# Second part's first RMS norm: the factor per token moved from the inputs of the 14 products to their sums

## The chip, the cores and the metric

The kernel runs on one core of a Trainium2 chip, as one launch. The metric is the device time of that launch in microseconds (us), lower is better. All arithmetic is on 32-bit floats; a product "in three passes" splits both operands into a high part (fp32r) and a low rest and adds high·high, high·low and low·high.

## The reference, cut to what matters

256 tokens of width 1024 pass a first block (a mixer and a feed-forward layer, ended by a layer norm "ln2") and then a second block. The change concerns the hand-over:

```python
x = _layer_norm(ALPHA * h + ff, ln2_g, ln2_b)            # end of the first block
...
def rmsnorm(x, g):
    return x * lax.rsqrt(jnp.mean(x * x, axis=-1, keepdims=True) + EPS) * g
h = rmsnorm(x, g_norm1) * (1.0 + sc1) + sh1              # sc1, sh1: one value per feature
proj = h @ w_in                                          # 1024 x 1792: 14 blocks of 128 outputs
q, k, v, z = jnp.split(proj, ...)                        # 4, 1, 1 and 8 blocks
q = rmsnorm(q, g_q); k = rmsnorm(k, g_k)                 # per head; then rotation and attention
z = gelu(z)                                              # then a token-mixing layer
```

rsqrt(mean) is one factor r per token. So proj = r · (x·gain) @ w + sh1 @ w, where gain = g_norm1·(1+sc1).

## The kernel before, in words

Activations lie transposed in SBUF: features on the 128 partitions in 8 tiles, tokens along the free dimension. `xh` and `xl` are the high and low parts of a product's input, 8 tiles of 16 + 256 columns (the 16 were the meta tokens of the first block and are free in the second). All weights come as one stream of 128x1024 blocks, issued by SP through a ring of four slots: `raw` is what landed, ACT's `hi(b)` (L1082 to L1089) rounds it to `wh`, DVE's `lo(b)` (L1605 to L1610) makes `wl = raw - wh`, and PE's `block` (L750 to L762) runs 24 matmuls of 256 columns. `hi(b)` waits until block b-4 is done on PE, `lo(b)` waits for `hi(b)`, PE waits for `lo(b)`. Both are written AHEAD = 3 blocks before their use. There is no planner: each engine's order is written out by hand, and each engine works strictly in that order.

The stage in question, with n counting the 14 blocks of `w_in` (B_IN2 to B_OUT2):

- **Layer norm ln2.** Statistics per token (L1947 to L1975, L1300 to L1317), PE turns the normed rows back to feature layout in banks 4 to 7 (L738).
- **RMS norm, before.** ACT squares each tile (L1371), PE sums the squares with eight full matmuls (L804) that spread the sum over all partitions, DVE makes x·gain from PSUM (L2025), ACT takes the root (L1382), DVE the reciprocal `spread` (L2028), then for each tile DVE multiplies by it (L2038), ACT adds the shift into `xh` (L1387), DVE makes `xl` (L2033).
- **Blocks 0 and 1** run tile by tile in `first_blocks` (L507). Blocks 2 to 13 run in `block`, in PSUM banks 0 and 1 in turn.
- **Between them**, PE transposes `res` (L818) and the token-mixing weights (L810), and does parts of attention and of the token-mixing layer (L835 to L933).
- **ACT's loop** (L1459 to L1503): iteration n is `hi(n+3)`, some extras, then, once block n is done, GELU (n < 8), a copy (n = 8), or a square and a scaled copy (n > 8), all read from PSUM.
- **DVE's loop** (L2115 to L2169): iteration n is extras, `lo(n+3)`, and for n < 8 one multiply-add of `ada` over 128x1024 (L1989), which computes a later modulation vector. In iteration 3 it also copies `y_tm` (L2149) and makes a diagonal (L2152). It doesn't read the blocks' sums.

Of the kernel before, what the change touches and what calls it, by code (L numbers as in the profile page):

```python
# [5 lines left out]
F32 = mybir.dt.float32  # L6
# [6 lines left out]
P = 128  # L13
# [17 lines left out]
QT = 4  # L31
# [99 lines left out]
def two_blocks(nc: bass.Bass, A: dict, out: bass.AP):  # L131
    with ExitStack() as ctx:
# [3 lines left out]
        def sem(name):  # L136
# [146 lines left out]
        q_scale = hb[:, 16:32].rearrange("p (i t h) -> p i t h", i=QT, t=NT)  # L283
        heads2 = cst[:, C_BLK:C_BLK + P:HD]
# [21 lines left out]
            "z_act", "zv_turned", "zv_copied", "zv_ms", "zv_std", "zv_n", "mixed", "tok_pre", "tok_done", "tok_sq",  # L306
# [8 lines left out]
        NORM = {what: sem(f"r1_{what}") for what in ("sq", "var", "std", "h", "hi", "lo")}  # L315

        def norm(what, n=1):
# [4 lines left out]
                   "norm_act": (0, 0, 3, 6), "turned": (0, 8, 16, 24), "h": (0, 8, 16, 16), "hi": (0, 8, 16, 24), "lo": (0, 8, 16, 16)}  # L322
# [144 lines left out]
        def _(pe):  # L467
# [282 lines left out]
            def block(b, bank, name, value, t=0, h=xh, l=xl, first=META):  # L750
# [5 lines left out]
                for n in range(KD):  # L756
                    a, z = h[:, n, first:first + SEQ], l[:, n, first:first + SEQ]
                    w_hi, w_lo = (w[:, b % RING, n * P:(n + 1) * P] for w in (wh, wl))
                    for w, x in ((w_hi, a), (w_hi, z), (w_lo, a)):
                        mm = nc.tensor.matmul(ps[:, bank, 0:SEQ], w, x, start=(k == 0), stop=(k == 3 * KD - 1))  # L760
                        k += 1
# [45 lines left out]
            pe.wait_ge(S["mixing_landed"], 64)  # L807
            for n in range(2):
                for q in range(4):
                    mm = nc.tensor.transpose(ps[:, 2 + n, q * P:(q + 1) * P], ws[:, 4 * n + q, :], ident)  # L810
                mm.then_inc(S["ws_turned"], 1)


            def turn_y(t):

                pe.wait_ge(*ln("n2", "hi", KD))
# [145 lines left out]
            for b in range(B_IN2, B_OUT2):  # L962
                n = b - B_IN2
                c = n - 2
                if c < 0:
                    free = (None, 0)
                elif c < 2 * QT:
                    free = ("z_act", c + 1)
                elif c == 2 * QT:
                    free = ("v2_ev", 1)  # L970
                else:
                    free = ("q_ev", c - 2 * QT)
# [9 lines left out]
                if n == 5:  # L982
                    gate_row()
# [93 lines left out]
        def _(act):  # L1077
# [287 lines left out]
            token_norm("n2", F1_BANKS, eps[:, 1:2], B_IN2 - 1 + AHEAD)  # L1365
            for m in range(KD):
                bank, at = turned_at("n2", m)
                act.wait_ge(*ln("n2", "turned", turns_needed(m)))
                if m >= 2:
                    act.wait_ge(*norm("h", m - 1))  # L1370
                nc.scalar.activation(sq[:, m, :], ps[:, bank, at:at + SEQ], ACT.Square, bias=col("ln2_b", m),  # L1371
                                     scale=col("ln2_g", m)).then_inc(NORM["sq"], 1)

            def n2_out(m):

                bank, at = turned_at("n2", m)
                act.wait_ge(*norm("h", KD if m < 4 else m + 1))
                nc.scalar.activation(y[:, m, :], ps[:, bank, at:at + SEQ], ACT.Identity, bias=col("ln2_b", m),
                                     scale=col("ln2_g", m)).then_inc(LN["hi"], 1)

            act.wait_ge(*norm("var"))
            nc.scalar.activation(std[:, :], ps[:, 1, 0:SEQ], ACT.Sqrt, bias=eps[:, 2:3]).then_inc(NORM["std"], 1)  # L1382
            n2_out(0)
            n2_out(1)
            for m in range(KD):
                act.wait_ge(*norm("h", KD + m + 1))
                nc.scalar.activation(xh[:, m, META:TOK], tg_m[:, m, :], ACT.Identity, bias=mod[:, M_SH1 + m:M_SH1 + m + 1])\  # L1387
                    .then_inc(NORM["hi"], 1)
                if m < KD - 2:
                    n2_out(m + 2)  # L1390
            for n in range(2):
                act.wait_ge(S["ws_turned"], n + 1)
                nc.scalar.copy(wst[:, 4 * n:4 * n + 4, :].rearrange("p h q -> p (h q)"), ps[:, 2 + n, :]).then_inc(S["ws_copied"], 1)
# [65 lines left out]
            for b in range(B_IN2, B_OUT2):  # L1459
                n = b - B_IN2  # L1460
                hi(b + AHEAD)
# [27 lines left out]
                act.wait_ge(blk_done, b + 1)  # L1489
                p_ = ps[:, b % 2, 0:SEQ]  # L1490
                if n < 2 * QT:
                    nc.scalar.activation((zv if n < QT else zu)[:, n % QT, :], p_, ACT.Gelu_apprx_tanh).then_inc(S["z_act"], 1)
                elif n == 2 * QT:
                    nc.scalar.copy(vv[:, :], p_).then_inc(S["v2_ev"], 1)
                else:
# [5 lines left out]
                    nc.scalar.activation(qs[:, t % 3, :], p_, ACT.Square)  # L1501
# [965 lines left out]
```

## Time and profile before

| what | us |
|---|---|
| median of 3 runs (808.5 to 810.74) | 808.83 |
| the profiled execution, its own time | 810.1 |
| its span | 808.3 |
| PE busy in the span | 767.9 (95%) |
| DVE busy | 577.1 (71%) |
| ACT busy | 464.3 (57%) |

The span is what the hardware profiler saw; the 1.8 us around it belong to the launch. A time forecast by a change of the span adds to 810.1, and the median lies 1.3 us below that. DMA engines were busy between 3% and 98% of a 10 us slice, and the mean granted TensorE clock was 0.983 of full speed.

### The profile page before, as it was taken

The numbers are of one execution on the slowest core, as the hardware profiler recorded it, in microseconds if no ns is written. First come the engines' busy times: TensorE is split into PE (matmuls) and PEld (weight loads), VectorE is DVE, ScalarE is ACT, GpSimd is POOL, SyncE is SP. The second block draws the span as 40 slices with busy tenths as digits, with TensorE's granted clock in tenths as the row PEclk, the third lists the DMA queues.
The fourth block names the chain that finished last, engine by engine and source line by source line (L and its number), as shares of the span: only waits on it lengthen the run. The fifth ranks groups of instructions, "written<-read, shape, count | busy, mean of one in ns | idle before, by whom it ended". The sixth has DMA issues, their size and how long they took to land.

```text
span 808.3 us, 14469 instructions
## 1 busy us (share of the span) xinstructions
PE 767.9 (95%) x5365; PEld 701.7 (87%) x5365; DVE 577.1 (71%) x852; ACT 464.3 (57%) x758; POOL 133.7 (17%) x139
## 2 busy tenths in 40 slices
PE   3999999999899989999999997999979999999996
PEld 2899999888899878899989995999868999999994
DVE  6896778753487576777584757888677798966676
ACT  4677564456675556544554536657856555555554
POOL 4000000000113204223232220000001312234321
PEclk9999999999999999999999999999997999999999
DMA  7354333225344577788777880573234676555641
GB/s 280 118 174 137 126 128 106 79 72 174 121 140 174 182 285 256 246 318 291 247 274 267 271 300 28 184 285 105 79 104 135 210 253 210 171 196 186 200 135 52
DMA packets 45863, 147.49 MB, mean 182 GB/s; under 512 B 9308, under 2 KB 10076, under 8 KB 45808
## 3 DMA queue, kind: packets, MB, share of 16 engines
q1 hardware_dynamic: 44544, 144.88, 52.7%
q10 hardware_dynamic: 1264, 1.86, 0.7%
q8 instruction: 36, 0.59, 0.3%
q14 instruction: 19, 0.16, 0.1%
HBM read 144.59 MB, written 1.05 MB: 180 GB/s over the span
## 4 chain that ended last, share of the span: by engine, by line
PE 90%; ACT 4%; DVE 4%; issue 1%; DMA 1%; DVEq 0%; POOL 0%; SPq 0%; ACTq 0%
PE ps L760 30%; PE ps L491 20%; PE ps L710 20%; PE ps L507 4%; PE ps L1013 1%; PE ps L770 1%; PE ps L558 1%; PE ps L684 1%; PE ps L572 1%; PE ps L951 1%; PE ps L587 1%; PE ps L527 1%; DMA vtk<-in_x 1%; PE ps L625 1%; ACT wh L1089 1%
## 5 line engine op out<-in xcount | busy, mean ns | idle before, releaser
L1610 DVE TENSOR_TENSOR wl<-raw,wh 128x1024 fp32r<-128x1024 f32 x220 | 282.5, 1288 | 131.1 <-ACT wh L1089 130.1
L1089 ACT ACTIVATE wh<-raw 128x1024 fp32r<-128x1024 f32 x220 | 231.6, 1054 | 66.0 <-PE ps L710 52.5
L760 PE MATMUL ps<-xh,wh 128*128 128x256 f32 x672 | 190.9, 284 | 1.5 <-DVE taps L2236 1.3
L760 PE MATMUL ps<-xh,wl 128*128 128x256 f32 x672 | 188.8, 281 | 0.0
L760 PE MATMUL ps<-xl,wh 128*128 128x256 f32 x672 | 188.8, 281 | 0.0
L760 PEld LDWEIGHTS ps<-xh,wh 128*128 128x128 f32 x672 | 127.3, 189 | 4.9 <-DVE taps L2236 1.5
L760 PEld LDWEIGHTS ps<-xl,wh 128*128 128x128 f32 x672 | 127.3, 189 | 2.3 <-issue 0.2
L760 PEld LDWEIGHTS ps<-xh,wl 128*128 128x128 f32 x672 | 127.4, 190 | 0.0
L491 PE MATMUL ps<-xh,wh 128*128 128x256 f32 (+1 forms) x400 | 117.7, 294 | 1.2 <-POOL xl L2303 1.0
L491 PE MATMUL ps<-xh,wl 128*128 128x256 f32 (+1 forms) x400 | 114.1, 285 | 0.0
L491 PE MATMUL ps<-xl,wh 128*128 128x256 f32 (+1 forms) x400 | 113.9, 285 | 0.0
L491 PEld LDWEIGHTS ps<-xh,wh 128*128 128x128 f32 x400 | 76.1, 190 | 4.2 <-issue 2.3
L491 PEld LDWEIGHTS ps<-xl,wh 128*128 128x128 f32 x400 | 76.2, 190 | 0.2
L491 PEld LDWEIGHTS ps<-xh,wl 128*128 128x128 f32 x400 | 76.1, 190 | 0.0
L2335 POOL TENSOR_TENSOR taps<-taps 128x256 f32<-128x256 f32 x22 | 23.9, 1087 | 239.4 <-ACT taps L1553 142.9
L710 PE MATMUL ps<-wh,gl 128*128 128x512 f32 x200 | 62.8, 395 | 0.0
L710 PE MATMUL ps<-wh,gh 128*128 128x512 f32 x200 | 62.8, 395 | 0.0
L710 PE MATMUL ps<-wl,gh 128*128 128x512 f32 x200 | 62.8, 395 | 0.0
L1548 ACT ACTIVATE taps<-ps,cols 128x256 f32<-128x256 f32 x44 | 24.8, 565 | 58.4 <-PE ps L760 53.5
L1989 DVE SCALAR_TENSOR_TENSOR ada_acc<-ada_w,silu_c,ada_acc 128x1024 f32<-128x1024 f32 x42 | 55.9, 1330 | 0.3
L1343 ACT ACTIVATE relu<-ps,cols 128x256 f32<-128x256 f32 x32 | 15.2, 476 | 60.8 <-PE ps L760 58.2
L2322 POOL TENSOR_TENSOR relu<-relu 128x256 f32<-128x256 f32 x32 | 21.3, 665 | 149.5 <-ACT relu L1343 149.5
(405 smaller groups left out, 1290.8 us busy)
## 6 DMA issues: line engine op xcount, KB each, us to landing
raw<-in_w_stream SPq DMA_DIRECT2D x220, 512.0 KB, 3.6
ada_w<-in_w_ada SPq DMA_DIRECT2D x48, 512.0 KB, 5.5
vtk<-in_x SPq DMA_DIRECT2D x2, 512.0 KB, 4.5
out<-ob SPq DMA_DIRECT2D x4, 256.0 KB, 2.0
u<-uT SPq DMA_DIRECT2D x16, 34.0 KB, 2.2
eepp<-in_s_mats SPq DMA_DIRECT2D x1, 512.0 KB
bti<-btr SPq DMA_DIRECT2D x16, 32.0 KB, 2.5
ws<-in_w_s ACTq DMA_DIRECT2D x1, 512.0 KB, 5.3
```

What stands on the lines that cost most here:

```text
L491: mm = nc.tensor.matmul(bank[:, 0:n], w, a, start=(k == 0), stop=(k == 3 * len(pieces) - 1))
L507: mm = nc.tensor.matmul(ps[:, banks[n], 0:TOK - first], w, x, start=(m == 0 and q == 0), stop=(m == KD - 1 and q == 2))
L527: mm = nc.tensor.transpose(ps[:, LN0_BANK[k], a:z], xt[n][0:z - a, k * P:(k + 1) * P], ident[0:z - a, 0:z - a])
L710: mm = nc.tensor.matmul(ps[:, banks[t][half], :], x, w[:, b % RING, half * 512:(half + 1) * 512], start=(first and n == 0), stop=False, sk ...
L760: mm = nc.tensor.matmul(ps[:, bank, 0:SEQ], w, x, start=(k == 0), stop=(k == 3 * KD - 1))
L1089: nc.scalar.activation(wh[:, b % RING], raw[:, b % RING], ACT.Identity).then_inc(hi_done, 1)
L1343: nc.scalar.activation(relu[:, j % 2, :], ps[:, up_bank(j), 0:SEQ], ACT.Relu, bias=bias).then_inc(S["f_relu"], 1)
L1548: nc.scalar.activation(dst[:, j % 2, :], ps[:, bank, 0:SEQ], ACT.Identity, bias=bias, scale=w)\
L1610: V.tensor_tensor(wl[:, b % RING], raw[:, b % RING], wh[:, b % RING].bitcast(F32), ALU.subtract).then_inc(lo_done, 1)
L1989: ins = V.scalar_tensor_tensor(acc, w, sc[:, k:k + 1], acc, ALU.mult, ALU.add)
L2322: G.tensor_tensor(relu2[:, j % 2, :], relu[:, j % 2, :], relu[:, j % 2, :], ALU.mult).then_inc(pool_step, 1)
L2335: G.tensor_tensor(cg[:, j % 2, :], ca[:, j % 2, :], cb[:, j % 2, :], ALU.mult).then_inc(S["ff2_g"], 1)
```

## The change

The factor r is no longer applied to the inputs. `xh`, `xl` are made from x·gain at once, while the squares are still being summed; the shift sh1 stands in columns 14 and 15 of the operand, so that each matmul has 258 columns and the sums of column 0 are sh1 @ w. DVE then does `scaled(n)`: copy of the shift sum, and sum times `spread` into `tg_m`; ACT reads `tg_m` with the shift as its bias. The sums of squares are four matmuls of 32 output rows side by side, in two rounds, and one more that adds them up and spreads them. Blocks 2 and 3 go to banks 2 and 3. In the excerpt below `shift` has been copied into columns 14 and 15 of `xh` and `xl` beforehand.

```diff
@@ tensor
-                    a, z = h[:, n, first:first + SEQ], l[:, n, first:first + SEQ]
+                    a, z = h[:, n, first:TOK], l[:, n, first:TOK]
...
-            for m in range(KD):
-                pe.wait_ge(*norm("sq", m + 1))
-                mm = nc.tensor.matmul(ps[:, 1, 0:SEQ], ones, sq[:, m, :], start=(m == 0), stop=(m == KD - 1))
-            mm.then_inc(NORM["var"], 1)
...
+            def sum_squares(half):
+
+                pe.wait_ge(*norm("sq", 4 * half + 4))
                 for q in range(4):
+                    mm = nc.tensor.matmul(ps[32 * q:32 * q + 32, 4, 0:SEQ], ones[:, 0:32], sq[:, 4 * half + q, :],
+                                          start=(half == 0), stop=(half == 1), skip_group_check=True)
+                mm.then_inc(NORM["parts"], 1)
+
+            def spread_sums():
+
+                pe.wait_ge(*norm("copied"))
+                nc.tensor.matmul(ps[:, 5, 0:SEQ], ones, qrot[:, :], start=True, stop=True).then_inc(NORM["var"], 1)
...
             def turn_y(t):
 
-                pe.wait_ge(*ln("n2", "hi", KD))
+                pe.wait_ge(*norm("std"))
+                pe.wait_ge(S["ws_copied"], 2)
...
                 if n == 0:
-                    first_blocks(b, (b % 2, (b + 1) % 2), lambda q: norm("lo", q + 1))
-                elif n >= 2:
-                    block(b, b % 2, *free)
-                if n in (1, 2):
-                    turn_y(n - 1)
+                    first_blocks(b, (0, 1), lambda q: ln("n2", "lo", q + 1), META - 2)
+                    sum_squares(0)
+                elif n in (2, 3):
+                    block(b, n, None, 0, first=META - 2)
+                elif n >= 4:
+                    block(b, n % 2, "z_scaled", max(c + 1, n - 3) if n >= 6 else n - 3, first=META - 2)
+                if n == 2:
+                    sum_squares(1)
+                    turn_ws()
+                    spread_sums()
+                if n in (3, 4):
+                    turn_y(n - 3)
...
-                if n == 5:
+                if n == 6:
                     gate_row()
@@ scalar
             token_norm("n2", F1_BANKS, eps[:, 1:2], B_IN2 - 1 + AHEAD)
+            split("n2", y, lambda m: col("ln2_g", m), lambda m: col("ln2_b", m))
+            act.wait_ge(*ln("n2", "h", KD))
             for m in range(KD):
...
+                nc.scalar.activation(sq[:, m, :], y[:, m, :], ACT.Square).then_inc(NORM["sq"], 1)
+            hi(B_IN2 + AHEAD)
+            act.wait_ge(*norm("parts", 2))
+            nc.scalar.copy(qrot[:, :], ps[:, 4, 0:SEQ]).then_inc(NORM["copied"], 1)
             for n in range(2):
                 act.wait_ge(S["ws_turned"], n + 1)
...
+            act.wait_ge(*norm("var"))
+            nc.scalar.activation(std[:, :], ps[:, 5, 0:SEQ], ACT.Sqrt, bias=eps[:, 2:3], scale=32.0).then_inc(NORM["std"], 1)
...
                 n = b - B_IN2
-                hi(b + AHEAD)
+                if n:
+                    hi(b + AHEAD)
...
-                act.wait_ge(blk_done, b + 1)
-                p_ = ps[:, b % 2, 0:SEQ]
+                act.wait_ge(S["z_scaled"], n + 1)
+                p_, shift = tg_m[:, n % KD, :], z_shift[:, n:n + 1]
                 if n < 2 * QT:
-                    nc.scalar.activation((zv if n < QT else zu)[:, n % QT, :], p_, ACT.Gelu_apprx_tanh).then_inc(S["z_act"], 1)
+                    nc.scalar.activation((zv if n < QT else zu)[:, n % QT, :], p_, ACT.Gelu_apprx_tanh, bias=shift).then_inc(S["z_act"], 1)
...
@@ vector
+            def gained_low(m):
+
+                dve.wait_ge(*ln("n2", "hi", m + 1))
+                V.scalar_tensor_tensor(xl[:, m, META:TOK], y[:, m, :], gain[:, 0, m:m + 1], xh[:, m, META:TOK].bitcast(F32),
+                                       ALU.mult, ALU.subtract).then_inc(LN["lo"], 1)
+
             for m in range(KD):
...
+                dve.wait_ge(*ln("n2", "h", m + 1))
+                V.tensor_scalar(xh[:, m, META:TOK], y[:, m, :], gain[:, 0, m:m + 1], None, ALU.mult).then_inc(LN["hi"], 1)
+                if m:
+                    gained_low(m - 1)
+            gained_low(KD - 1)
+            lo(B_IN2 + AHEAD)
             dve.wait_ge(*norm("std"))
             step(V.reciprocal(spread, std[:, :]))
...
+            def scaled(n):
+
+                dve.wait_ge(blk_done, B_IN2 + n + 1)
+                if n >= KD:
+                    dve.wait_ge(S["z_act"], n - KD + 1)
+                bank = n if n < 4 else n % 2
+                if n > 2 * QT:
+                    V.tensor_scalar(z_shift_g[:, n - 2 * QT - 1:n - 2 * QT], ps[:, bank, 0:1], col("g_q" if n > 2 * QT + 1 else "g_k"), None, ALU.mult)
+                V.tensor_copy(z_shift[:, n:n + 1], ps[:, bank, 0:1])
+                V.tensor_tensor(tg_m[:, n % KD, :], ps[:, bank, 2:2 + SEQ], spread, ALU.mult).then_inc(S["z_scaled"], 1)
...
             for n in range(B_OUT2 - B_IN2):
+                if n:
+                    scaled(n - 1)
...
-                lo(B_IN2 + n + AHEAD)
+                if n:
+                    lo(B_IN2 + n + AHEAD)
                 for r in ada_rows(n):
                     ada(r, 1)
-                if n == 3:
+                if n == 5:
                     dve.wait_ge(S["y_turned"], NT)
...
+            scaled(B_OUT2 - B_IN2 - 1)
```

The old steps L1371 to L1390 on ACT and L2025, L2031 to L2042 on DVE are gone.

## Rows read from the trace of the kernel before

**Rows 1.** Timeline of PE (start, us, what, idle before it).
```profile
492.43 1.09 PE L738 MATMUL ps<-cst,sq 128*128 128x128 f32 x8 [1.59 <-DVE sq L1973]
...
502.36 0.58 PE L507 MATMUL ps<-xh,wh 128*128 128x256 f32 x1 [3.08 <-DVE xl L2033]
...
539.92 1.97 PE L845 MATMUL ps<-wst,zvt 128*64 128x128 f32 x32
...
563.70 0.48 PE L1013 MATMUL ps<-wh,mh 128*128 128x512 f32 x1
```
**Rows 2.** Busy time by stretch (PE, PEld, DVE, ACT, POOL); granted clock, DMA share, GB/s.
```profile
502.00:508.40 6.40, 6.04 (x28) 6.05 (x29) 5.71 (x14) 6.26 (x16) 0.00 (x0) 0.50 0.01 1
511.00:563.70 52.70, 52.70 (x432) 49.74 (x430) 45.58 (x75) 31.86 (x62) 0.00 (x0) 0.97 0.61 220
```
**Rows 3.** The chain that ended last, 470 to 600 us: start, us, what.
```profile
498.94 1.76 DVE small L2028
...
502.36 8.67 PE ps L507 x48
...
515.59 5.68 PE ps L760 x48
...
545.33 0.43 PE ps L871 x2
```
**Rows 4.** Timelines of PE and of DVE at the first block's other layer norm.
```profile
296.31 1.10 PE L738 MATMUL ps<-cst,sq 128*128 128x128 f32 x8 [1.58 <-DVE sq L1973]
298.52 0.38 PE L507 MATMUL ps<-xh,wh 128*128 128x256 f32 x1 [1.12 <-DVE xl L1643]
...
299.46 0.29 DVE L1648 CAST xh<-res 128x256 fp32r<-128x256 f32 x1
299.66 0.42 DVE L1643 TENSOR_TENSOR xl<-res,xh 128x256 fp32r<-128x256 f32 x1
```
**Rows 5.** Timeline of DVE in the stage.
```profile
510.55 0.75 DVE L1987 TENSOR_SCALAR ada_acc<-ada_w,silu_c 128x1024 f32<-128x1024 f32 x1
...
514.41 1.22 DVE L1610 TENSOR_TENSOR wl<-raw,wh 128x1024 fp32r<-128x1024 f32 x1
515.55 1.28 DVE L1989 SCALAR_TENSOR_TENSOR ada_acc<-ada_w,silu_c,ada_acc 128x1024 f32<-128x1024 f32 x1
516.75 1.21 DVE L1610 TENSOR_TENSOR wl<-raw,wh 128x1024 fp32r<-128x1024 f32 x1
...
545.80 0.42 DVE L2058 TENSOR_TENSOR qrot<-ps,rope 128x256 f32<-128x256 f32 x1
...
551.49 1.67 DVE L2134 SCALAR_TENSOR_TENSOR ml<-zu,cols,mh 128x256 fp32r<-128x256 f32 x4
...
557.73 0.16 DVE L2080 SCALAR_TENSOR_TENSOR smax<-smax,hb 128x2 f32<-128x2 f32 x1
557.81 0.68 DVE L2079 TENSOR_REDUCE smax<-ps 128x2 f32<-128x512 f32 x1
...
558.61 1.22 DVE L1610 TENSOR_TENSOR wl<-raw,wh 128x1024 fp32r<-128x1024 f32 x1
```
**Rows 6.** Timeline of ACT in the stage.
```profile
510.70 0.38 ACT L1492 ACTIVATE zv<-ps 128x256 f32<-128x256 f32 x1
510.99 1.05 ACT L1089 ACTIVATE wh<-raw 128x1024 fp32r<-128x1024 f32 x1
...
546.88 1.34 ACT L1477 ACTIVATE sq<-zu 128x256 f32<-128x256 f32 x4
```
**Rows 7.** Waits of DVE from 509 to 563 us: total, times, longest.
```profile
DVE qrot L2058 <- PE ps L871: 2.9, 2, 2.1
DVE wl L1610 <- ACT wh L1089: 2.4, 3, 1.4
DVE vtok L2118 <- PE ps L865: 1.7, 1, 1.7
DVE zv L2121 <- PE ps L845: 0.5, 1, 0.5
```

More of the change, by code:

```diff
@@ L311, in two_blocks @@
         )}
-        NORM = {what: sem(f"r1_{what}") for what in ("sq", "var", "std", "h", "hi", "lo")}
+        NORM = {what: sem(f"r1_{what}") for what in ("sq", "parts", "copied", "var", "std")}
         def norm(what, n=1):
@@ L756, in block @@
                 for n in range(KD):
-                    a, z = h[:, n, first:first + SEQ], l[:, n, first:first + SEQ]
+                    a, z = h[:, n, first:TOK], l[:, n, first:TOK]
                     w_hi, w_lo = (w[:, b % RING, n * P:(n + 1) * P] for w in (wh, wl))
                     for w, x in ((w_hi, a), (w_hi, z), (w_lo, a)):
-                        mm = nc.tensor.matmul(ps[:, bank, 0:SEQ], w, x, start=(k == 0), stop=(k == 3 * KD - 1))
+                        mm = nc.tensor.matmul(ps[:, bank, 0:TOK - first], w, x, start=(k == 0), stop=(k == 3 * KD - 1))
                         k += 1
@@ L1500, in _ @@
                         act.wait_ge(S["b3_full"], ROTATED[t - 3])
[L1501 to L1502 removed]
+                    nc.scalar.activation(qs[:, t % 3, :], p_, ACT.Square, bias=shift)
+                    nc.scalar.activation(qg[:, t % 3, :], p_, ACT.Identity, bias=z_shift_g[:, t:t + 1], scale=col("g_q" if t else "g_k"))\
                         .then_inc(S["q_ev"], 1)
@@ L2017, in _ @@
             step(V.scalar_tensor_tensor(gain[:, 0, :], mod[:, M_SC1:M_SC1 + KD], 1.0, span("g_norm1"), ALU.add, ALU.mult))
-            step(V.tensor_tensor(gain[:, 2, :], gain[:, 0, :], span("ln2_g"), ALU.mult))
-            step(V.tensor_tensor(gain[:, 3, :], gain[:, 0, :], span("ln2_b"), ALU.mult))
+            shift = mod[:, M_SH1:M_SH1 + KD, None].to_broadcast([P, KD, 2])
+            shift_hi, shift_lo = (x[:, :, META - 2:META] for x in (xh, xl))
+            step(V.tensor_copy(shift_hi, shift))
@@ L2024, in _ @@
-                dve.wait_ge(*norm("sq", m + 1))
-                V.tensor_scalar(tg_m[:, m, :], ps[:, bank, at:at + SEQ], gain[:, 2, m:m + 1], gain[:, 3, m:m + 1], ALU.mult, ALU.add)\
-                    .then_inc(NORM["h"], 1)
+                dve.wait_ge(*ln("n2", "h", m + 1))
[3 more added lines that the diff above has]
+            gained_low(KD - 1)
@@ L2027, in _ @@
+            lo(B_IN2 + AHEAD)
             dve.wait_ge(*norm("std"))
             step(V.reciprocal(spread, std[:, :]))
-            def r1_low(m):
-                dve.wait_ge(*norm("hi", m + 1))
-                V.scalar_tensor_tensor(xl[:, m, META:TOK], tg_m[:, m, :], mod[:, M_SH1 + m:M_SH1 + m + 1], xh[:, m, META:TOK].bitcast(F32),
-                                       ALU.add, ALU.subtract).then_inc(NORM["lo"], 1)
-            dve.wait_ge(*norm("h", KD))
-            for m in range(KD):
-                V.tensor_tensor(tg_m[:, m, :], tg_m[:, m, :], spread, ALU.mult).then_inc(NORM["h"], 1)
-                dve.wait_ge(*norm("h", KD + m + 1))
-                if m:
-                    r1_low(m - 1)
```

52 lines of the change are left out of this document (12 added, 40 removed).

## The prediction

> **What bounds the kernel now.** I read the table first (PE busy 95% of the span, DVE 71%, ACT 57%), then the chain that ended last, then the three engines' timelines from 490 to 600 us. The chain is PE nearly everywhere. The stretch that matters to the change has two parts. From 490 to 502 us PE has too little to do: the first product of block 0 starts at 502.36 after 3.08 us of idleness that ends with DVE's `xl` [rows 1]. By then the granted clock has fallen: 0.50 from 502.0 to 508.4 us, which is the 1.2 GHz level [rows 2], so blocks 0 and 1 take 8.67 us for 48 matmuls where blocks 3 and 4 take 5.68 [rows 3]. From 511.0 to 563.7 us PE is busy for all 52.7 us; DVE is busy for 45.6 of these and ACT for 31.9 [rows 2]. DVE's load is the number to remember: it has 7 us to spare in 52.7.
>
> **Part 1: the norm leaves the path in front of block 0.** After the change `xh` and `xl` need only the layer norm's output, ACT's `split` and two DVE steps per tile. The same structure stands at the other layer norm: PE's last transposes start at 296.31, the first product at 298.52, 2.21 us later [rows 4]. Here those transposes start at 492.43 [rows 1], so the first product starts at 494.65; `xl` is now a three-operand step, some 0.06 longer: 494.7. That is 7.7 us earlier. The DVE step for `xh` is a multiply by a column from SBUF to SBUF, which no row shows at 256 columns. Bounds: the cast, 0.20 from start to start [rows 4], and a pass from PSUM, 0.42 [rows 5]. With 0.40 for `xl` (four of that form in 1.67, the last one 0.48) [rows 5] a tile costs DVE 0.60 to 0.82 against PE's six matmuls of 0.118 [rows 3], 0.71 us. I take 0.22, nearest in kind to the cast, and PE sets the pace: blocks 0 and 1 end at about 500.5 (upper bound: 0.9 later). The Trainium skill ("VectorE: DVE Perf Modes", Why PSUM operands drop a tier) says a 32-bit operand in PSUM is held to one result per cycle while a one-tensor step from SBUF may give two; by it the lower bound holds, as taken. The clock: at the other norm PE had the same gaps, 1.58 and 1.12 us, and its first product took 0.38 [rows 4] where here it took 0.58 [rows 1]; so I count on full speed. Blocks 0 and 1 thus end 10.5 us earlier than 511.0.
>
> **Part 2: what PE gains in work.** The sums of squares are two rounds of four matmuls 32 outputs wide. Wholly one after the other, a round would cost four times 0.43 [rows 3], 1.7 us; wholly side by side 0.43. The nearest row is L845: 16 matmuls 64 outputs wide (32 instructions, 128 columns) in 1.97 us [rows 1], 0.12 each, where half of the 0.43 for 256 columns at full width is 0.21. I take 0.5 per round. The Trainium skill ("TensorEngine Tiling (Array Packing)", When to Use Tiling) gives a factor of four at this width; by the factor of two in the row it would be 0.9 per round and 0.8 us later in all. Then the spreading matmul, 0.45, and the eight transposes of `ws`, 0.9, which lay in the idle stretch before and now lie on PE's path. The two extra columns: a block of 24 matmuls of 256 takes 2.84 [rows 3]; in proportion two more are 0.02 per block, 0.3 in all, and not less than nothing. Nothing for the rest of ACT's work: eight reads (at most half of a `hi` that is four times as wide, 0.5), eight squares of 0.34 and `hi(3)` of 1.05 [rows 6] end at 500.7, before PE asks for the last squares at 503.9.
>
> So PE: round one 500.5 to 501.0, block 2 to 503.9, round two, `ws`, spreading (behind ACT's copy, covered by `ws`) to 505.9 with its tail. ACT's root ends at 506.5, DVE's reciprocal takes 1.76 [rows 3] and `spread` is there at 508.3. Until then DVE has stood still since 501.7, in front of 2 us of work that it could have done.
>
> **Part 3: the new order of DVE and ACT.** `scaled(n)` costs DVE a small copy (0.08 from start to start) and a PSUM pass of 0.42 [rows 5], so 0.50 until ACT can start; 0.08 more for n > 8. What counts is what stands behind it. ACT's GELU of block n waits for `scaled(n)`. ACT's next instruction is `hi(n+4)`. DVE's next after `scaled(n)` is `lo(n+4)`, which waits for that `hi`. So in every iteration DVE waits while ACT does a GELU (0.28 to the next start) and a `hi` (1.05) [rows 6], with two hops 1.43 us, and then does `lo` 1.14 and `ada` 1.20, from start to start [rows 5]. The period is 0.50 + 1.43 + 1.14 + 1.20 = **4.27 us**, against 2.9 for a block on PE. Before, neither engine waited for the other beyond `hi` to `lo`, and DVE's share was 2.34 per iteration.
>
> First consequence: block 4 waits for `lo(4)`. DVE: `ada` 0.67 (short, first), `scaled(0)` to 509.5, ACT to 510.9, `lo(4)` done at 512.1; PE is ready at 509.4 and idles 2.7 us. Next, the transposes of `zv` wait for GELU of block 3, about 522.6, and the gate row for DVE's copies and diagonal, about 534.3.
>
> The end of the stage by DVE's own sum, from 508.3. Its old work from `ada` at 510.55 to the end of the last `lo` (558.61 + 1.14 = 559.75) [rows 5] spans 49.2 us, less the waits in it: 0.8 of the 2.9, 1.0 of the 2.4 (the other parts lie outside), 1.7 and 0.5 [rows 7], 4.0: 45.2. Without the last `lo`, 44.1. New: thirteen `scaled` ahead of it, 6.8. New waits: nine iterations of 1.43, 12.9; in the last four the extras cover most of the wait for `hi`, but DVE waits for a root, for ACT's `mh` and for PE's rotation; each lies between nothing and 1.43, I take 1 for each, 3. Sum 66.8, so the maxima of the scores are done at 575 (before: 558.6). From there to the first product of the next stage it took 5.1 us before, with the end of block 13 in between; after, block 13 is done by then and only exponentials, scores and the turning of probabilities are left: I take 4 (5.1 as the bound): 579 against 563.70 [rows 1]. **The stage ends 15.3 us later.** Beyond it the order is as before and PE bound, so it stays. SP's weight loads wait for `lo(b-4)`; they come later too, but have four periods to land, so nothing waits for a DMA.
>
> The clock on this path: PE idles for 3 to 7 us before block 5 and again near 568, so I expect 1.2 GHz there; PE is ahead of DVE by more than a block's 2.3 us extra, and nothing is added, except that block 13, which stands in front of the scores, may cost up to 2.3 more. Before, the mean clock of the 52.7 us was 0.97 [rows 2], so some of this is in the 563.70 too. Bounds 0 and 2.3; I take 0, because the exponentials overlap it.
>
> Sum: the profiled execution took 810.1, so 825.4; the median stands 1.3 below: **824**.
>
> **The rivals.**
> - *DVE and ACT keep pace (faster).* Place: the wait of `lo(n+4)` for `hi(n+4)`. If the two waits of 1.43 fell away, DVE would need 0.50 + 2.34 = 2.84 per block, just under PE's 2.9, and the stage would stay PE bound. It decides at a period of 2.9. Then PE's sum counts: 7.7 for the start and 2.9 for the clock, less 2.3 for sums, spreading and `ws`, less 0.3 for columns: 8.0 us, 801 on the median. For: PE was busy throughout and ACT had 20 us to spare. Against: the order in the code puts `hi` behind the GELU. The Trainium skill ("TensorEngine Tiling (Array Packing)", PSUM Bottleneck) advises both ScalarE and VectorE for emptying PSUM, which speaks for this outcome; here both touch every block, one behind the other.
> - *The lock-step is partly hidden.* If DVE's waits were 0.7 instead of 1.43, or half of them fell to PE's lateness, 6 to 7 us would go: 817.
> - *The clock falls before 494.7.* For: it fell by 502 here. Against: the other norm. Price: up to 48 matmuls at 0.213 instead of 0.118, 4.6 us, from the ratio of the two levels and 0.118, passed on whole through the reciprocal: 828.6.
> - *The sums don't run side by side*, so the change doesn't save what it says: 2 times 1.2 us later: 826.4.
>
> **How the numbers follow.** My forecast with its own range, 819 to 829: 0.62. Partly hidden: 0.12. Clock or sums (slower too): 0.12. Kept pace: 0.10. Even (a gain and a loss of 8 that cancel): 0.04. The range of 8 in 10 leaves out the keeping of pace and the even case: 813 to 831. A measurement here tells 0.3%, 2.4 us, from no change. Faster 0.10, same 0.04, slower 0.86.
>
> **What would show it.** Right: first product at 494.7; `small` ready near 508.3; idle PE in front of block 4 ended by DVE's `wl`; from there a wait of about 1.4 us of DVE for ACT `wh` in nearly every iteration, and of ACT for DVE `tg_m`; starts of the `tg_m` steps 4.3 us apart up to the fifth; the first matmul of L1013's successor 15 us later than 563.7. Wrong: DVE without those waits, blocks 2.9 us apart, or the first products at 0.21 us each.

## The result and the profile after

| what | before | after |
|---|---|---|
| median of 4 runs each, us | 808.72 | 831.11 (827.84 to 834.82) |
| ratio after to before, 95% interval | | 1.0273 [1.0226, 1.0319] |
| profiled execution, its span | 810.1, 808.3 | 831.22, 829.4 |
| mean granted clock | 0.983 | 0.973 |

The changed kernel is 2.7% slower. The forecast was 824 with a range of 813 to 831. Its sign is right; its size is at the very end of the range, with four runs that lie between 828 and 835, and outside the narrower range of 819 to 829 that was given the chance of 0.62. (The profiled execution before, 810.1, is not one of the four runs.)

To find the place, take two marks that both kernels have: PE's last normed transposes ahead of the stage [rows 1], and the first matmul of the next stage's product, L1013 before [rows 1] and L1024 after. PE's timeline of the kernel after (start, us, what, idle before it) at both marks and at the first product:

```profile
495.19 1.09 PE L739 MATMUL ps<-cst,sq 128*128 128x128 f32 x8 [1.59 <-DVE sq L1969]
...
497.53 0.39 PE L508 MATMUL ps<-xh,wh 128*128 128x258 f32 x1 [1.24 <-DVE xl L2023]
...
585.05 0.48 PE L1024 MATMUL ps<-wh,mh 128*128 128x512 f32 x1
```

Before, the stage lasts 563.70 - 492.43 = 71.3 us; after, 585.05 - 495.19 = 89.9: 18.6 more. Ahead of the stage the run is 2.76 us late, behind it 0.25 us less is needed. 2.8 + 18.6 - 0.3 = 21.1, the difference of the spans.

Inside the stage, the waits of PE in the kernel after, 495 to 586 us (waiting group, releaser: total, times, longest):

```profile
PE ps L847 <- ACT zv L1488: 5.2, 1, 5.2
PE ps L839 <- DVE ws L2157: 3.5, 1, 3.5
PE ps L761 <- DVE wl L1606: 2.7, 1, 2.7
PE ps L883 <- DVE kf L2142: 1.9, 1, 1.9
PE ps L899 <- ACT qstd L1470: 1.9, 1, 1.9
```

These are what DVE and ACT owe PE: the last of the GELU results that are transposed (`zv`), the gate row's diagonal, a low half, the key, a root. Before, PE was busy from 511.0 to 563.7 without a wait [rows 2]. The same view for DVE names the cause:

```profile
DVE wl L1606 <- ACT wh L1100: 14.9, 10, 1.5
DVE small L2034 <- ACT std L1388: 5.6, 1, 5.6
```

Ten waits for ACT's high half stand where three with 2.4 us in all stood before [rows 7]: one of 1.2 us at 501.8 us, ahead of the reciprocal, and nine of 1.52 us in the periods that follow. A period in DVE's timeline of the kernel after shows how they arise:

```profile
512.36 0.41 DVE L2045 TENSOR_TENSOR tg_m<-ps,small 128x256 f32<-128x256 f32 x1
514.29 1.23 DVE L1606 TENSOR_TENSOR wl<-raw,wh 128x1024 fp32r<-128x1024 f32 x1 [1.52 <-ACT wh L1100]
515.43 1.28 DVE L1985 SCALAR_TENSOR_TENSOR ada_acc<-ada_w,silu_c,ada_acc 128x1024 f32<-128x1024 f32 x1
516.62 0.15 DVE L2044 COPY hb<-ps 128x1 f32<-128x1 f32 x1
516.69 0.42 DVE L2045 TENSOR_TENSOR tg_m<-ps,small 128x256 f32<-128x256 f32 x1
```

and ACT's timeline over the same stretch has the other half:

```profile
512.80 0.51 ACT L1488 ACTIVATE zv<-tg_m,hb 128x256 f32<-128x256 f32 x1 [1.71 <-DVE tg_m L2045]
513.22 1.04 ACT L1100 ACTIVATE wh<-raw 128x1024 fp32r<-128x1024 f32 x1
517.14 0.51 ACT L1488 ACTIVATE zv<-tg_m,hb 128x256 f32<-128x256 f32 x1 [2.89 <-DVE tg_m L2045]
517.56 1.04 ACT L1100 ACTIVATE wh<-raw 128x1024 fp32r<-128x1024 f32 x1
```

Read them together in order of time: DVE scales (to 512.77), ACT does GELU (512.80) and then its high half (513.22 to 514.26), DVE only then its low half (514.29) and the multiply-add, and only then scales again (516.69). But for overlaps of a few hundredths of a us at the hand-overs, one of the two engines works at any time. The chain that ended last runs through these same steps for 40 us (start, us, what):

```profile
517.56 1.05 ACT wh L1100
518.67 1.11 issue
519.78 1.28 DVE ada_acc L1985
```

"issue" is time without a visible wait; here it is DVE's low half, as the timeline shows.

### The profile page after: what moved, and what is told of

Read it like the earlier page. It is cut to its first block, busy times and chain, and to the rows that moved or that the text cites. A ratio compares the mean times of both kernels' runs of the same rounds, so it can differ in the third digit from the quotient of the medians.

```text
span 829.4 us, 14483 instructions
## 1 busy us (share of the span) xinstructions
PE 774.4 (93%) x5367; PEld 706.9 (85%) x5367; DVE 579.0 (70%) x877; ACT 462.4 (56%) x751; POOL 134.3 (16%) x139
## 4 chain that ended last, share of the span: by engine, by line
PE 84%; DVE 7%; ACT 5%; issue 3%; DMA 1%; DVEq 0%; POOL 0%; SPq 0%; ACTq 0%
PE ps L761 26%; PE ps L492 20%; PE ps L711 19%; PE ps L508 3%; ACT wh L1100 2%; PE ps L1024 1%; DVE ada_acc L1985 1%; PE ps L771 1%; PE ps L559 1%; PE ps L685 1%; PE ps L573 1%; PE ps L963 1%; PE ps L588 1%; DVE wl L1606 1%; PE ps L528 1%
## 5 line engine op out<-in xcount | busy, mean ns | idle before, releaser
L761 PE MATMUL ps<-xh,wh 128*128 128x256 f32 (+1 forms) x672 | 193.7, 288 | 4.8 <-DVE wl L1606 2.7
L761 PE MATMUL ps<-xl,wh 128*128 128x256 f32 (+1 forms) x672 | 191.3, 285 | 0.0
L761 PE MATMUL ps<-xh,wl 128*128 128x256 f32 (+1 forms) x672 | 191.0, 284 | 0.0
L761 PEld LDWEIGHTS ps<-xh,wh 128*128 128x128 f32 x672 | 129.6, 193 | 9.3 <-issue 4.4
L761 PEld LDWEIGHTS ps<-xl,wh 128*128 128x128 f32 x672 | 129.6, 193 | 2.3 <-issue 0.2
L761 PEld LDWEIGHTS ps<-xh,wl 128*128 128x128 f32 x672 | 129.7, 193 | 0.0
L492 PE MATMUL ps<-xh,wh 128*128 128x256 f32 (+1 forms) x400 | 117.7, 294 | 1.2 <-POOL xl L2309 1.0
L492 PE MATMUL ps<-xh,wl 128*128 128x256 f32 (+1 forms) x400 | 114.0, 285 | 0.0
L492 PE MATMUL ps<-xl,wh 128*128 128x256 f32 (+1 forms) x400 | 113.9, 285 | 0.0
L492 PEld LDWEIGHTS ps<-xh,wh 128*128 128x128 f32 x400 | 76.1, 190 | 4.2 <-issue 2.3
L492 PEld LDWEIGHTS ps<-xl,wh 128*128 128x128 f32 x400 | 76.1, 190 | 0.3
L492 PEld LDWEIGHTS ps<-xh,wl 128*128 128x128 f32 x400 | 76.1, 190 | 0.0
L711 PEld LDWEIGHTS ps<-wl,gh 128*128 128x128 f32 x200 | 37.5, 187 | 9.2
```

The costliest lines, as they stand in the source:

```text
L492: mm = nc.tensor.matmul(bank[:, 0:n], w, a, start=(k == 0), stop=(k == 3 * len(pieces) - 1))
L711: mm = nc.tensor.matmul(ps[:, banks[t][half], :], x, w[:, b % RING, half * 512:(half + 1) * 512], start=(first and n == 0), stop=False, sk ...
L761: mm = nc.tensor.matmul(ps[:, bank, 0:TOK - first], w, x, start=(k == 0), stop=(k == 3 * KD - 1))
```

## The experiments

Ten kernels, in three groups; each group has its own runs of the kernel before beside it (medians 810.14, 809.25 and 809.01 us), so the ratios are what to compare. "Stage" is the time between the two marks in the profiled execution.

| kernel | median, us | ratio [95%] | stage, us |
|---|---|---|---|
| before | 808.72 | 1 | 71.3 |
| after | 831.11 | 1.0273 [1.0226, 1.0319] | 89.9 |
| hi_first | 815.52 | 1.0061 [1.0039, 1.0084] | 74.8 |
| no_ada | 823.07 | 1.0154 [1.0126, 1.0183] | 82.5 |
| before_step | 817.26 | 1.0076 [1.0050, 1.0101] | 77.7 |
| before_step_wait | 827.95 | 1.0212 [1.0182, 1.0241] | 88.4 |
| after_early | 822.88 | 1.0164 [1.0140, 1.0188] | 84.8 |
| early_spread | 811.60 | 1.0028 [1.0016, 1.0041] | 74.1 |
| early_all | 812.25 | 1.0026 [1.0006, 1.0047] | 74.1 |
| filler | 830.24 | 1.0256 [1.0240, 1.0271] | 89.7 |
| kf_only | 809.51 | 0.9994 [0.9976, 1.0013] | 72.0 |
| best | 806.47 | 0.9973 [0.9959, 0.9987] | 67.4 |

### Group 1: is it the lock-step?

The theory: the loss is the order in which DVE and ACT wait for each other. The rival: it is the added work, the 14 scaling steps and the wider products, wherever they stand.

**hi_first**: the kernel after, with ACT's next high half ahead of the wait. Nothing is added or removed.

```diff
@@ ACT's loop over the blocks
-                if n:
-                    hi(b + AHEAD)
...
+                if b < B_OUT2 - 1:
+                    hi(b + 1 + AHEAD)
                 act.wait_ge(S["z_scaled"], n + 1)
```

> The changed kernel with one order altered: in ACT's loop the rounding hi(n+4) stands ahead of the wait for scaled(n), not behind the GELU; the computation is the same. Theory (lock-step): DVE's lo(n+4) no longer waits for a GELU that waits for DVE, so its wait of 1.52 us per iteration goes, the scaled steps come 2.8 to 3.0 us apart and not 4.3, and the next stage's first product comes some 16 us earlier: 813 to 817. Rival 1 (DVE simply has 0.5 us more work per block): the order changes nothing, 829 to 832. Rival 2 (the clock, fallen in PE's idle stretches, is the price): the gaps close with the waits, but where the gaps stay the time stays above 822.

Measured: 815.52, ratio 1.0061, the stage 15.1 us shorter with all the work still there. DVE's waits in hi_first, 495 to 586 us:

```profile
DVE small L2034 <- ACT std L1388: 7.1, 1, 7.1
DVE qrot L2060 <- PE ps L883: 2.9, 3, 1.8
DVE hb L2043 <- PE ps L761: 1.3, 1, 1.3
DVE wl L1606 <- ACT wh L1100: 1.2, 1, 1.2
```

The nine waits of 1.52 us are gone; the one that is left, 1.2 us, is the one ahead of the reciprocal. The scaling steps come 2.73 us apart (expected: 2.8 to 3.0). Some four fifths of the loss (15.1 of the 18.6 us of the stage, and 2.1 of the 2.7%) was the place of one instruction.

**no_ada**: the kernel after, with the stage's eight `ada` steps narrowed to 8 of 1024 columns. It leaves out most of a modulation vector of the second half.

```diff
-            def ada(n, acc_, t=0):
+            def ada(n, acc_, t=0, width=D):
...
-                    ada(r, 1)
+                    ada(r, 1, width=8)
```

> The changed kernel without the eight multiply-adds of ada over 1024 columns in DVE's loop of the stage (8 columns of each are kept for the semaphores; the second half's scale vector is thereby not computed). Theory (lock-step): the period falls by the 1.2 us of ada alone, to 3.1 or 3.2, since the wait for ACT stays at 1.5; eight iterations bring 8 to 9 us: 821 to 823, and DVE still waits 1.5 us for ACT's wh in each iteration. Rival 1 (too much DVE work): DVE's load per block is then 1.7 us, far under PE's 2.9, PE bounds the stage again: 810 to 815. Rival 2 (clock): between the two, with no wait of DVE for wh.

Measured: 823.07, 8.0 below the kernel after, and still "DVE wl <- ACT wh" of 14.9 us in ten waits. The first scaling steps come 3.29 us apart (expected: 3.1 to 3.2) and not 4.34. Taking some 9 us of DVE's work out (0.67 and seven times 1.20) shortens the stage by 7.4; so most of this work lies on the path, although in the kernel after DVE is idle for 27.5 of the 90 us from 495 to 585. That is what a serial chain looks like. If DVE merely had too much work, it would not wait for ACT at all.

**before_step_wait** and **before_step**: the kernel before, with the scaling step's work on DVE for each block (into a buffer that nobody reads). In the first ACT waits for it as in the kernel after; in the second it doesn't, DVE does it after ACT's read of the block. PE waits for it in both, since the bank is read.

```diff
@@ DVE, for each block n
+                V.tensor_copy(hb[:, 32 + n:33 + n], ps[:, n % 2, 0:1])
+                V.tensor_tensor(tg_m[:, n % KD, :], ps[:, n % 2, 0:SEQ], spread, ALU.mult).then_inc(S["z_scaled"], 1)
@@ ACT, before_step_wait alone
-                act.wait_ge(blk_done, b + 1)
+                act.wait_ge(S["z_scaled"], n + 1)
```

> As the one before, but DVE's step comes first and ACT's reading of the block (still from PSUM) waits for it, as in the change. Theory (lock-step): the waits alone bring the loss, with blocks 0 and 1 as late as before: 17 to 18 us over before, 825 to 829, with DVE waiting 1.4 us for ACT's wh in each iteration. Rival 1: the same time as without the wait.

> The kernel before with the DVE step of the change added and nothing else: per block a copy of one column and a product with spread into tg_m, at the same place in DVE's order, after ACT has read the block; ACT does not wait for it, its result is not used. Theory (lock-step): work alone costs little, DVE has the slack: 0 to 5 us over before, by the hand schedule 4: 809 to 814. Rival 1 (too much DVE work): 15 or more: 823 and above.

Measured: 827.95 with the wait, as expected; 817.26 without, above the expected 809 to 814. The kernel before, with nothing of the new norm in it, loses 17 us of stage time by the step and ACT's wait alone, and has the same signature (DVE `wl` waits for ACT `wh`, 14.0 us in ten waits). So the new arithmetic on PE is not the cause. Of the 17.1 us ACT's wait makes 10.6. Without it 6.4 remain, not 0 to 5: here PE must wait until two engines one after the other have read a bank (3.8 us in two waits for DVE `tg_m`), it waits 1.1 us for the key, and the first scores and block 13 take 0.7 us more than before. That part I had priced too low; what else is in the 6.4 was not traced.

### Group 2: what is left of it?

hi_first is still 0.6% above the kernel before. DVE stands still for 7.1 us before `spread` in it, just before it has too much to do.

**early_spread**: hi_first with both rounds of sums, the `ws` transposes and the spreading product ahead of block 2, and on ACT the root ahead of the two copies of `ws`. **early_all**: in addition DVE's first four `ada` steps stand ahead of its wait for the root. **after_early**: all of these edits on the kernel after, with ACT's loop unchanged. The loop leaves the four `ada` steps out where they stand ahead of it.

```diff
@@ PE, n == 0
                     sum_squares(0)
+                    sum_squares(1)
+                    turn_ws()
+                    spread_sums()
@@ PE, n == 2
-                    sum_squares(1)
-                    turn_ws()
-                    spread_sums()
@@ ACT, all three
+            act.wait_ge(*norm("var"))
+            nc.scalar.activation(std[:, :], ps[:, 5, 0:SEQ], ACT.Sqrt, bias=eps[:, 2:3], scale=32.0).then_inc(NORM["std"], 1)
             for n in range(2):
                 act.wait_ge(S["ws_turned"], n + 1)
...
-            act.wait_ge(*norm("var"))
-            nc.scalar.activation(std[:, :], ps[:, 5, 0:SEQ], ACT.Sqrt, bias=eps[:, 2:3], scale=32.0).then_inc(NORM["std"], 1)
@@ DVE, early_all and after_early alone
             lo(B_IN2 + AHEAD)
+            for n in range(4):
+                for r in ada_rows(n):
+                    ada(r, 1)
             dve.wait_ge(*norm("std"))
```

> As early_all without the four moved multiply-adds: only the sums, the `ws` transposes and the spreading product stand ahead of block 2. Lock-step theory: `spread` is ready about 3.5 us after the first blocks end and not 7 to 8, so DVE begins to scale some 3 to 4 us earlier, of which part is lost where the products wait for other things: 812.5 (811 to 815). Rival: the start does not count, since DVE catches up by the end of the stage anyway: 815 to 816, as hi_first.

> The kernel after with ACT's next high half ahead of its wait (as in hi_first), with DVE's first four multiply-adds of the scale vector ahead of its wait for the root of the sums, and with the second four sums, the `ws` transposes and the product that spreads the sums ahead of block 2. Lock-step theory: DVE's standing still before `spread` (7.1 us in hi_first) goes nearly to nothing, it reaches the blocks about 3 us earlier and has 4 x 1.2 us less to do between them. The products' waits in the stage of hi_first (zv 3.5, `kf` 1.8, gate 1.6, low halves 1.1, 8 us in all) shrink to 2 or less, so the time is 808 (805 to 811), at or below the kernel before. Rival (the change's own extra work, not its order, is what is left of the loss): the 14 scaling steps stay on DVE's path and it stays within 1.5 us of hi_first, 814 to 816.

> The kernel after with ACT's order left as it is, but with the early sums and the four early multiply-adds. Lock-step theory: `spread` comes about 1 us earlier (DVE's four multiply-adds end 4.3 us after its last low half) and four periods of 4.35 us lose their 1.2 us, so the time is 826 (824 to 828); the wait of DVE for ACT's high half stays at 1.4 to 1.5 us each in the periods. Rival (what costs is ACT's order in a few early periods only): with the head start gone, the loss is gone and the time is below 820.

Measured: early_spread 811.60, in its range. But the profiled stage is only 0.7 us shorter than in hi_first, and the intervals of the two ratios just meet; the gain is not well settled. Its first scores and block 13 took 6.5 us (2.01 and 4.45), where they took 5.6 in hi_first (1.33 and 4.31), with PE at its low clock for part of it in both; without that difference the stage would be some 1.5 us shorter than in hi_first, an estimate. after_early, at 822.88, lies below its expected 824 to 828: it gained 8.2 us in the median and 5.1 in the stage; the ten waits for ACT are all there, 14.9 us. (An offset ahead of the stage, 492.14 against 495.19 for the last transposes, is part of the surplus and not the edit's.) early_all missed: 812.25 where 808 was expected, and not below early_spread: moving four steps into idle time gave nothing that can be measured. Its waits, PE's and then DVE's, 496 to 580 and 575 us, show what took the place of DVE's standing still:

```profile
PE ps L839 <- DVE ws L2159: 3.2, 1, 3.2
PE ps L883 <- DVE kf L2144: 1.8, 1, 1.8
```

```profile
DVE ada_acc L1984 <- DMA ada_w<-in_w_ada: 2.5, 1, 2.5
```

The fifth `ada` step came before its data; DVE lost 2.5 us there, and PE 3.2 us later, at the gate row. And TensorE ran at its low level for part of this stretch late in the stage (stretch; busy us of PE; granted clock; DMA share; GB/s; early_all):

```profile
550.00:555.00 5.00, 4.18 (x36) 1.00 0.32 105
555.00:560.00 5.00, 3.99 (x14) 0.57 0.32 105
560.00:565.00 5.00, 5.00 (x32) 0.75 0.34 110
```

**filler**: the kernel after, with three products of 256 columns (measured: 1.46 and 1.58 us for the three) in PE's two late gaps, to see whether the standing still brings the clock down.

```diff
+            def filler():
+
+                for _ in range(3):
+                    nc.tensor.matmul(ps[:, 4, 0:SEQ], ident, cst[:, 0:SEQ], start=True, stop=True)
@@ q_stat(i), ahead of its wait
+                if i == 0:
+                    filler()
@@ q_stat(i), behind its matmuls
+                if i == 1:
+                    filler()
```

> The kernel after with three products into a bank that is free, about 1.3 us of work each time, in the two places where TensorE stands still late in the stage (before the key's statistics, 1.87 us, and before the second rotation, 1.90 us). If the low clock of 575 to 580 (scores of the first two heads 2.01 us, block 13 4.12 us) comes from the standing still just before it, the granted clock is then 0.9 or more there, block 13 takes 2.9, and the time is 829 (827.5 to 830.5). Rival (the clock falls at this point for another reason): block 13 stays at 4.1 and the time at 831 or above.

Measured: 830.24, in its range, but not to be told from the kernel after (ratios 1.0256 [1.0240, 1.0271] and 1.0273 [1.0226, 1.0319]). The same view for the kernel after and then for filler:

```profile
565.00:570.00 5.00, 4.99 (x29) 0.69 0.12 26
570.00:575.00 5.00, 3.10 (x26) 0.84 0.21 79
575.00:580.00 5.00, 5.00 (x18) 0.50 0.30 105
```

```profile
565.00:570.00 5.00, 4.68 (x36) 1.00 0.26 78
570.00:575.00 5.00, 3.57 (x22) 0.77 0.16 46
575.00:580.00 5.00, 5.00 (x23) 0.54 0.22 86
```

Behind the first gap, filled to all but 0.57 us, the clock stayed up (0.69 to 1.00). Behind the second it fell as before, but there the key came late too, so that 1.43 us of standing still remained. The test is inconclusive: it doesn't tell whether a fuller gap would have held the clock. Block 13 took 3.96 us, against 4.12 in the kernel after and the 2.9 of the theory. The kernel before tells more. PE had no wait there from 511.0 to 563.7 us, and yet its clock fell behind the first scores (PE's chain; then stretch, PE busy, clock, DMA share, GB/s):

```profile
555.40 1.10 PE ps L918 x8
556.50 4.47 PE ps L760 x24
```

```profile
555.00:560.00 5.00, 5.00 (x27) 0.66 0.31 105
```

So standing still just before is not needed for the fall at this place, and the low clock of block 13 is not a price of the change.

### Group 3: can the waits that are left be taken away?

**kf_only**: early_all, with one low half moved behind the copy of the swapped key, on which PE waited 1.8 us. **best**: in addition the diagonal's eight steps move from period 5 to period 3, into the time in which DVE waited for `ada` data.

```diff
@@ DVE, n == 13
                     bank3_read(V.tensor_copy(kf[:, 1, :], ps[:, 3, 0:SEQ]))
+                    lo(B_IN2 + 12 + AHEAD)
@@ DVE
-                if n:
+                if n and n != 12:
                     lo(B_IN2 + n + AHEAD)
@@ DVE, best alone
+                if n == 3:
+                    dve.wait_ge(S["ws_turned"], 2)
+                    for m in range(KD):
+                        V.tensor_scalar(diag[:, m * P:(m + 1) * P], ident, mod[:, M_GT1 + m:M_GT1 + m + 1], float(D), ALU.mult, ALU.mult)\
+                            .then_inc(S["row_diag"], 1)
                 if n == 5:
...
-                    dve.wait_ge(S["ws_turned"], 2)
-                    for m in range(KD):
-                        V.tensor_scalar(diag[:, m * P:(m + 1) * P], ident, mod[:, M_GT1 + m:M_GT1 + m + 1], float(D), ALU.mult, ALU.mult)\
-                            .then_inc(S["row_diag"], 1)
```

> As early_all, with one low half (the one of period 12) moved on DVE behind the copy of the swapped key. In early_all TensorE stood still 1.83 us for that copy, and the granted clock was 0.57 and 0.75 in the two 5 us behind it (scores 2.08 us where the kernel before has 1.17, block 13 about 4.3 us where 2.9 is usual). If the low clock follows the standing still, both go: the wait falls under 0.7 us, scores take 1.2, block 13 2.9, and TensorE begins the next stage 3 to 4.5 us sooner after its last normed transposes than the 74.1 us of early_all: the run at 807.5 to 809. Rival (the clock falls there whatever the wait): only the 1.2 to 1.8 us of the wait come back, 809.5 to 810.5.

> As kf_only, with the eight diagonal products (1.65 us on DVE, on which the gate's row waited 3.2 us in early_all) moved from period 5 to period 3, where DVE waited 2.5 us for data. If each wait that is taken away comes back in time, the gate's wait falls to about 1.3 and the run to 806 (804.5 to 808), 0.2 to 0.6% below the kernel before. Rival (DVE is behind by then, so that another wait takes the gate's place): the same as kf_only within 1 us.

Measured: kf_only 809.51, not to be told from the kernel before; it missed the 807.5 to 809 of the theory and lies at the lower end of what the rival gave. The place itself went as the theory had it: the wait for the key fell from 1.8 to 0.7, the scores took 1.14, block 13 3.0, and the clock stayed at 1.00 from 545 to 565. But the stage became only 2.1 us shorter. Part of the rest went at the gate row: its wait (3.4 us) was followed by the low clock for longer than in early_all (0.53 from 525 to 530 and 0.79 from 530 to 535, against 0.66 and 1.00), so that from the gate row's product to the one of `zvt` (L857) 15.5 us passed and not 14.3. In best, without that wait, the clock stayed up at this place. The stretch in kf_only and then in best (PE busy, clock, DMA share, GB/s):

```profile
525.00:530.00 5.00, 3.91 (x6) 0.53 0.61 220
```

```profile
525.00:530.00 5.00, 5.00 (x45) 1.00 0.85 288
```

best: 806.47, ratio 0.9973 [0.9959, 0.9987], in its expected range, its stage 3.9 us shorter than that of the kernel before. The rival, that another wait takes the gate's place, is out: best is 3.0 us below kf_only, where it gave at most 1. PE's waits in best, 496 to 566 us, are all of these:

```profile
PE ps L847 <- ACT zv L1487: 1.6, 1, 1.6
PE ps L883 <- DVE kf L2144: 0.8, 1, 0.8
```

and DVE's first periods there are 1.5 us long, without a wait:

```profile
508.55 0.41 DVE L2047 TENSOR_TENSOR tg_m<-ps,small 128x256 f32<-128x256 f32 x1
508.88 1.22 DVE L1605 TENSOR_TENSOR wl<-raw,wh 128x1024 fp32r<-128x1024 f32 x1
510.02 0.15 DVE L2046 COPY hb<-ps 128x1 f32<-128x1 f32 x1
510.09 0.41 DVE L2047 TENSOR_TENSOR tg_m<-ps,small 128x256 f32<-128x256 f32 x1
```

So the change does pay, by about 0.3% (a small effect, at an interval of 0.1 to 0.4%), once ACT's high half, the sums, four `ada` steps, the diagonal and one low half are put where hardly an engine waits for them. Such moves were not tried on the kernel before; PE waits for nothing there from 511.0 to 563.7 [rows 2], so they have no wait to take away in that stretch. That is an argument and not a run.

## Why the prediction was right, and what was mis-sized

**Part 1 (the norm leaves the path): right.** The first product came 497.53 - 495.19 = 2.34 us after the last transposes (predicted 2.27), and blocks 0 and 1 ran at full clock in 6.01 us on the chain, against 8.67 [rows 3]. The step `xh`, which no row of before showed, took 0.35 with 0.26 to the next start (taken: 0.22). The rival "clock falls before 494.7" did not come in this profile.

**Part 2 (PE's extra work): right.** The sums and the chain around them, kernel after:

```profile
503.54 0.57 PE ps L808 x8
504.11 3.05 PE ps L761 x24
507.15 0.57 PE ps L808 x8
...
509.83 1.77 DVE small L2034
```

A round of four (x8, two instructions to a matmul) took 0.57 (taken: 0.5). One after the other they would be 4 x 0.43 = 1.7 [rows 3], so they overlap; the rival "the sums don't run side by side" is out. The gain is a factor of 1.72 / 0.57 = 3.0, measured. The Trainium skill ("TensorEngine Tiling (Array Packing)", When to Use Tiling) gives four for 32 outputs; the trace shows less. `spread` was ready at 511.60, which is 508.8 on the predicted time line (less the 2.76), 0.5 later than the predicted 508.3.

**Part 3 (the period): right in mechanism, 0.07 short.** The first scaling steps start at 512.36, 516.69, 521.04, 525.38 and 529.73: 4.34 us apart (predicted 4.27, before_step_wait 4.22). PE idled 2.7 us in front of block 4, as predicted. The missing part is in GELU: it took 0.51 with 0.42 to the next start, where 0.38 and 0.28 had been read from a GELU that takes its input from PSUM without a bias [rows 6]. In before_step_wait, where it still reads PSUM, it took 0.38 and DVE's waits were 1.40 and not 1.52. The Trainium skill ("ScalarE: Activation LUTs", What ACT_TABLE_LOAD costs) puts one more operand by pointer, here the bias, at about 93 ns, and the Trainium skill ("Perfetto Trace Analysis", Optimizing Scalar/DVE Operations) an access to SBUF at 93 ns where one to PSUM is 51; together that is an estimate of 135 ns, and 130 to 140 were measured. The kernel before shows the first part by itself: of two neighbouring readings of the same bank, the one without a pointer took 0.38 (L1501 at 552.34) and the one with a scale by pointer 0.47 (L1502 at 552.62), 0.09 more. That leaves 0.04 to 0.05 for SBUF.

**The steps that were mis-sized: DVE's waits, and block 13 at the end of the stage ("block 13 is done by then ... I take 0").** The forecast of the stage was 15.3 us longer, and it was 18.6: 3.3 short. Of these 0.5 came with `spread` in part 2. Another 1.6 lie in DVE's own sum, from `spread` to the maxima: 68.4 us (511.60 to 580.00) against the 66.8 taken. The waits in it were 2.3 more: nine of 1.52 where 1.43 was taken (0.8), those for a root, for ACT's `mh` and for PE's rotation 1.3 each where 1 was taken (0.9), and one of 0.54 for PE's first scores, which had no term. The work came out 0.7 shorter.

The last 1.1 lie behind the maxima: 5.1 us to the next stage, where 4 was taken (5.1 as the bound). The chain of the kernel after behind 574 us:

```profile
574.99 1.22 PE ps L883 x2
576.20 2.01 PE ps L930 x8
578.21 4.12 PE ps L761 x24
```

Block 13 was not "done by then". In PE's order it stands behind the first scores, and it ended at 582.33, 2.3 us after the maxima at 580.00. The clock was 0.50 from 575 to 580, the 1.2 GHz level; block 13 took 4.12 where 3.0 is its time at full clock (kf_only). That difference is the 1.1 that the forecast put at nothing. The kernel before had the same: block 13 took 4.47 there (its lines stand with the run filler), it ended 2.3 us after the maxima as well, and 5.0 us passed from them to the next stage. Scores and block 13 together took 5.57 before and 6.13 after. So this end of the stage was wrongly shortened in the forecast; from the first scores to the end of block 13 the change made it only some 0.6 us longer.

**What no step covered.** The rest of the distance to 831, 3.7 us, lies outside the stage. The profiled run was 2.76 us late ahead of it. Nearly all of that arose at the first block's other norm, whose code is the same: its first product began 0.5 us later than before (299.00 against 298.52), the first product behind it 2.75 us later (307.38 against 304.63). The granted clock there (stretch, PE busy, clock, DMA share, GB/s), after and then before:

```profile
300.00:305.00 5.00, 5.00 (x29) 0.59 0.91 277
```

```profile
300.00:305.00 5.00, 4.79 (x41) 1.00 0.80 267
```

In the profiled executions of the twelve kernels the last transposes began anywhere from 492.14 to 495.48, and no relation to the edits is to be seen: after and after_early, whose code is the same up to there, are at 495.19 and 492.14. That the offset is chance and not the change's is likely by this, but one profile for each kernel doesn't show it. The other 1.2 us: the kernel after's median lies 0.1 below its profiled execution, not 1.3. Without these two the forecast would have been 3.1 us off; that the result still touches the range owes something to the range's width.

**The rivals.** "DVE and ACT keep pace" named the point that decides, the wait of `lo(n+4)` for `hi(n+4)` and a period of 2.9 against 4.27, and hi_first shows that price: 15.1 us of stage time for that wait. But without it the stage was still 3.5 us longer than before, where the rival had promised 8 less. PE's waits in hi_first (3.5 us for GELU's `zv`, 1.8 for the key, 1.6 for the gate row, 1.1 for a low half) show what it left out: DVE, having stood still for 7.1 us, was late at the places where PE waits for it. best, with these mended, comes to 3.9 less. The Trainium skill's advice ("TensorEngine Tiling (Array Packing)", PSUM Bottleneck) to empty PSUM with both ScalarE and VectorE doesn't say how; with one behind the other on the same block, as in before_step_wait, the run lost 2.1%.

The prediction's 0.213 us for a matmul at the low clock does not follow from the two levels and 0.118, as it says (that gives 0.236); it is the distance of starts in the kernel before's first products (502.74, 502.95, 503.16), so the price of 4.6 us stands. The rival did not come.

**What stays open.** What brings the clock down late in the stage. It fell behind waits of 1.90 us (after), 1.83 (early_all) and 0.79 (best, where the scores took 2.01), and stayed up behind 0.70 (kf_only); but it fell in the kernel before with no wait at all. Nor is it shown how much of early_spread's gain over hi_first is its own, or what the kernel before would gain by reordering.

## What to carry to other kernels

When a step is inserted on engine A whose result engine B awaits, look at what B does next and who waits for that: if A's next instruction needs it, the two engines take turns, the period is the sum of both engines' work, and no table of busy shares shows it (DVE 70%, ACT 56% here). The signature is the same wait, of the same length, in every period (nine of 1.52 us here); the remedy is to put B's independent work ahead of its wait, and it was worth 15 of 18.6 us here. Look also at the end of the stage in the trace of before: a clock that is low there is already in its time, and a forecast that builds this end anew must carry it. Work taken off the head of a stage then pays only if the engine that was freed there gets something to do, and what it is given must have its data.

## What the runs showed of the hardware that was not expected

- A GELU from SBUF with its bias by pointer took 0.51 us against 0.38 from PSUM without one, for the same 128x256 (0.09 of it is a pointer operand, by two readings of the kernel before); in a serial chain each block pays for it.
- Four sums of 32 outputs side by side take 0.57 us in full 32-bit floats, against 0.43 for one matmul of the same columns at full width.
- The granted clock fell while PE was busy without a gap: 0.66 from 555 to 560 us in the kernel before, with 5.00 of 5.00 us busy, and 4.47 us for a block that takes 2.8.
- The same code had a granted clock of 0.59 in one execution and 1.00 in another (300 to 305 us, above). The same mark lay up to 3.3 us apart in single profiles (492.14 to 495.48), more than several of the effects tested here. Stage times between two marks of the same profile are what to compare; the ratios over many runs have the last word.
